# Sample retention outputs with the masked queries as weights, four column quarters side by side, instead of the states as weights

## The reference, cut to what matters

```python
def step(s, qkv):
    qc, kc, vc = qkv
    scores = jnp.einsum('bhid,bhjd->bhij', qc, kc) * decay_mat
    o = (jnp.einsum('bhij,bhjd->bhid', scores, vc)
         + jnp.einsum('bhid,bhde->bhie', qc * q_decay, s))
    ...
mu = jnp.mean(o, axis=-1, keepdims=True)
var = jnp.mean(jnp.square(o - mu), axis=-1, keepdims=True)
o = ((o - mu) * lax.rsqrt(var + GN_EPS)).reshape(B, L, R) * gn_g
ret_out = jax.nn.silu(g) * o
mix = jnp.concatenate([pool_out, ret_out], axis=-1) @ w_out
```

## Time and profile before

| | |
|---|---|
| median of 3 runs | 827.15 us (826.68 to 827.21) |
| span of the profiled execution | 823.5 us |
| its own time | not given on the page; the median of the runs is 3.65 us above its span |
| TensorE busy | 808.6 us, 98% |
| VectorE, ScalarE, POOL busy | 73%, 58%, 39% |
| DMA | 188.18 MB, mean 229 GB/s |

### The profile page before, as it was taken

How to read it: one execution, slowest core, us unless ns; L and a number is a source line. 1 busy time by engine, 2 the same in 40 slices (tenths; PEclk the granted TensorE clock), 3 DMA queues, 4 the chain that set the end, 5 groups by cost and what they waited for, 6 DMA issues and landing times.

```text
span 823.5 us, 11871 instructions
## 1 busy us (share of the span) xinstructions
PE 808.6 (98%) x4070; PEld 651.3 (79%) x4070; DVE 600.6 (73%) x957; ACT 478.4 (58%) x810; POOL 320.3 (39%) x207
## 2 busy tenths in 40 slices
PE   9999999999999999999999999999999999999995
PEld 6887788888868888888588887888878678888871
DVE  5444655645689999999854456555747899999986
ACT  5533342513478888887663432442334798888874
POOL 0016994301042345664100299913011322665540
PEclk9999999999999999999999999999999999999999
DMA  9732223223949999998853222221278699999867
GB/s 308 269 111 77 71 71 115 92 76 130 411 169 359 382 354 382 395 375 295 267 194 101 73 78 76 64 90 65 84 285 328 207 416 359 382 384 391 339 234 281
DMA packets 57295, 188.18 MB, mean 229 GB/s; under 512 B 10862, under 2 KB 11886, under 8 KB 49036
## 3 DMA queue, kind: packets, MB, share of 16 engines
q1 hardware_dynamic: 44476, 156.57, 52.5%
q0 software_dynamic: 10368, 23.09, 7.6%
q10 hardware_dynamic: 2400, 7.87, 2.5%
HBM read 173.00 MB, written 29.39 MB: 246 GB/s over the span
## 4 chain that ended last, share of the span: by engine, by line
PE 90%; DVE 4%; DMA 3%; issue 1%; ACT 1%; POOL 0%; ACTq 0%; SPq 0%; POOLq 0%; DVEq 0%
PE ps L485 13%; PE ps L1455 12%; PE ps L1457 12%; PE ps L1456 12%; PE ps L489 10%; PE ps L488 10%; PE ps L1463 3%; PE ps L487 3%; PE ps L1434 2%; PE ps L1654 1%; PE ps L1715 1%; DMA hg<-xn_d,rowidx 1%; PE ps L1679 1%; PE ps L1694 1%; PE ps L1405 1%
## 5 line engine op out<-in xcount | busy, mean ns | idle before, releaser
L485 PE MATMUL ps<-wh,hT 128*128 128x512 f32 x408 | 163.5, 401 | 0.2
L898 POOL DMA_INDIRECT y_d<-y,rowidx x32 | 111.8, 3493 | 125.8 <-DVE y L2179 124.5
L2154 DVE TENSOR_TENSOR gul<-wgu,eh 128x1024 fp32r<-128x1024 f32 x128 | 150.1, 1212 | 0.1
L2145 DVE SCALAR_TENSOR_TENSOR wl<-raw,gcol,wh 128x512 fp32r<-128x512 f32 x80 | 78.5, 984 | 75.3 <-ACT wh L1107 75.2
L1138 ACT ACTIVATE eh<-wgu 128x1024 fp32r<-128x1024 f32 x128 | 128.4, 1058 | 3.7 <-PE ps L1457 3.7
L489 PE MATMUL ps<-wh,lT 128*128 128x512 f32 x313 | 122.4, 391 | 0.0
L488 PE MATMUL ps<-wl,hT 128*128 128x512 f32 x313 | 121.9, 390 | 0.0
L1455 PE MATMUL ps<-eh,hgTh 128*128 128x512 f32 x240 | 96.6, 403 | 0.4 <-issue 0.4
L1457 PE MATMUL ps<-eh,hgTl 128*128 128x512 f32 x240 | 93.9, 391 | 0.0
L1456 PE MATMUL ps<-gul,hgTh 128*128 128x512 f32 x240 | 93.6, 390 | 0.0
L1107 ACT ACTIVATE wh<-raw,gcol 128x512 fp32r<-128x512 f32 x80 | 57.3, 719 | 59.8 <-PE ps L487 57.6
(11 more groups left out here) (271 smaller groups left out, 1688.2 us busy)
## 6 DMA issues: line engine op xcount, KB each, us to landing
wgu<-in_gate_up SPq DMA_DIRECT2D x64, 1024.0 KB, 12.4
wdn<-in_w_down SPq DMA_DIRECT2D x64, 512.0 KB
raw<-in_w_in SPq DMA_DIRECT2D x79, 256.0 KB, 2.7
raw<-in_w_out SPq DMA_DIRECT2D x32, 256.0 KB, 2.9
back<-y_d SPq DMA_DIRECT2D x16, 512.0 KB, 5.5
s<-in_state_ret POOLq DMA_DIRECT2D x8, 512.0 KB, 4.0
xn_d<-xf ACTq DMA_DIRECT2D x8, 512.0 KB, 6.6
x_in<-in_x_cols SPq DMA_DIRECT2D x8, 288.0 KB, 5.2
```

The costliest lines, as they stand in the source:

```text
L485: pe.matmul(out, both, w_h, start=first, stop=False)
L898: pool.indirect_dma_start(out=y_d, out_offset=bass.IndirectOffsetOnAxis(ap=rowidx[:, 1, e:e + 1], axis=0), in_=y[s][:, :], in_offset=None, ...
L2145: ve.scalar_tensor_tensor(out=wl[S % SPL][:, :], in0=raw[S % RAW][:, :], scalar=gcol[:, 0, L, s % KC:s % KC + 1], in1=wh[S % SPL][:, :].bi ...
L2154: ve.tensor_tensor(gu_pair(gul, gul3, e, s, p), gu_pair(wgu, wgu3, e, s, p), gu_split(e, p)[:, :].bitcast(F32), ALU.subtract).then_inc(glo, 1)
```

## The change

The operands are swapped. Now the states stream (128 columns) and the queries are the stationary operand. To keep sequences apart, POOL builds qm: for each head and each half (32 tokens, 4 sequences) a strip of 160 zeros in which four groups of 8 query columns stand 40 apart. A window of 32 columns at 32b holds the queries of sequence b of the half at their own place and zeros elsewhere, so four products by four states add up in one output of 32 rows. A pair of heads with two halves each makes four such outputs; they go to partitions 0, 32, 64 and 96 of bank B_OT, 128 columns a pair of heads. The scores' product has the score tile (32 columns) as stationary operand and v streaming. The four outputs are taken in turn for each b.

The output then is in natural layout, tokens down. The copy on ScalarE and the transposes back are gone. Statistics take two instructions of each kind instead of four, on a tile that has heads 0 and 2 in rows 0 to 63 and heads 1 and 3 in rows 64 to 127; the norm writes them as 64 rows of four heads. The table gneps is arranged to match, and rows 64 to 127 of on[LAST] are zeroed once.

```diff
--- before.py
+++ after.py
@@ -87,6 +87,9 @@
     def row_eps(chunk):
         return EPS_GN * np.exp(-2.0 * ((p % chunk) + 1.0).astype(f)[:, None] * log_g[None])
 
+    def by_half(rows):
+        return np.concatenate([np.where(p[:, None] < NSAMP, rows[:, 0::2], rows[:, 1::2])] * 2, 1)
+
     def kdecay(chunk):
         return np.exp((chunk - 1.0 - (p % chunk)).astype(f)[:, None] * log_g[None]) * scale
 
@@ -106,7 +109,7 @@
         "decay": np.stack([decay(P), decay(DECS)], 1),
         "cosT": np.concatenate([np.cos(ang)[:, :LAST]] * 2, 2).transpose(2, 1, 0),
         "sinT": np.concatenate([np.sin(ang)[:, :LAST], -np.sin(ang)[:, :LAST]], 2).transpose(2, 1, 0),
-        "gneps": np.stack([row_eps(P), row_eps(DECS)], 1),
+        "gneps": np.stack([row_eps(P), by_half(row_eps(DECS))], 1),
         "kdec": np.stack([kdecay(P)] + [kdecay_sample(0 if L + 1 < NL else LATE) for L in range(NL)], 1),
         "seqm": seq_mask,
         "least": np.broadcast_to(np.where(valid > 0, f(3.5), f(9))[:, :, None], (P, NT, NG)),
@@ -184,6 +187,7 @@
         hT = tile("hT", [P, KC, TOK], F32R, off=region)
         lT = tile("lT", [P, KC, TOK], F32R, off=region + 20 * 1024)
         xT = tile("xT", [P, KC, TOK], off=region)
+        qm = tile("qm", [P, 2, 4, 160], off=region)
         hg = [tile(f"hg{i}", [P, D], off=region + 4096 * i) for i in range(3)]
         y = [tile(f"y{i}", [P, D], off=region + 4096 * (3 + i)) for i in range(3)]
         hgTh = tile("hgTh", [P, KC, P], F32R, off=region + 4096 * 6)
@@ -389,6 +393,14 @@
         def q_turned(h, t):
 
             return qT[:, h, 0:NSAMP] if t == LAST else z[:, h, OFFS["q"], t * P:(t + 1) * P]
+
+        def own_queries(h, half):
+
+            return qm[:, h // 2, 2 * (h % 2) + half, :].rearrange("p (b s) -> p b s", s=40)[:, :, 0:DECS]
+
+        def masked_queries(h, half, b):
+
+            return qm[:, h // 2, 2 * (h % 2) + half, 32 * b:32 * b + 32]
 
         def keys_there(L, t):
 
@@ -925,13 +937,21 @@
                 pool.wait_ge(zmm, 5 * NT * (L + 1))
                 for h in range(2, NH):
                     load_s0(L, h)
-
-                for t in range(NT):
+                link(pool.memset(qm[:, :, :, :], 0.0))
+
+                for t in range(2):
+                    gate_gain(L, t)
+                pool.wait_ge(qk_ev, keys_there(L, LAST))
+                for h in range(NH):
+                    for half in range(2):
+                        last = pool.tensor_copy(own_queries(h, half), qT[:, h, 32 * half:32 * half + 32].rearrange("p (b s) -> p b s", s=DECS))
+                last.then_inc(qm_done, 1)
+                for t in range(2, NT):
                     gate_gain(L, t)
                 for h in range(LATE, NH):
                     if h == 2:
                         pool.wait_ge(sg_done, NT * (L + 1))
-                        pool.wait_ge(o_back, L + 1)
+                        pool.wait_ge(o_mm, NT * L + LAST)
                     if h == 3:
                         pool.wait_ge(on_tr, NT * L + 5)
                     pool.tensor_tensor(vb[h][:, :, :], over(zq(LAST, "v")[:, h * P:(h + 1) * P], DECB),
@@ -1304,8 +1324,6 @@
                     w_hi(L, s)
                 sc.wait_ge(st_ready, LAST * (L + 1))
                 sc.dma_start(o["new_ret_prompt"][L], st[:, :, :]).then_inc(st_st, 16)
-                sc.wait_ge(o_mm, NT * (L + 1))
-                sc.activation(scT[1][:, :, :], heads(ps[B_OT][:, :]), ACT.Copy).then_inc(o_ev, 1)
                 w_hi(L, WIN_STEPS + 8)
                 o_hi(sc, L, 0)
                 o_hi(sc, L, 1)
@@ -1700,21 +1718,29 @@
                     last = pe.matmul(ps[B_KV][:, h * P:(h + 1) * P], kd[t % 2][:, h, :], zq(t, "v")[:, h * P:(h + 1) * P], start=True, stop=True)
                 last.then_inc(kv_mm, 1)
 
-            def sample_part(L, h, part):
-
-                out = ps[B_OT][:, h * P:(h + 1) * P]
-                if h == 0 and part == 0:
+            def sample_heads(L, hp):
+
+                if hp == 0:
                     pe.wait_ge(sc_ev, NT * (L + 1))
                     pe.wait_ge(kd_done, NT * (L + 1))
                     for t in (2, 3, LAST):
                         z_there(pe, L, 4, t)
-                if part == 0:
+                    pe.wait_ge(qm_done, L + 1)
+                for h in (2 * hp, 2 * hp + 1):
                     pe.wait_ge(s0_ld[h], 16 * (L + 1))
-                    pe.matmul(out, zq(LAST, "v")[:, h * P:(h + 1) * P], scT[0][:, h, :], start=True, stop=False)
-                for b in (2 * part, 2 * part + 1):
-                    last = pe.matmul(out[:, b * DECS:(b + 1) * DECS], s0[h][:, b, :], qT[:, h, b * DECS:(b + 1) * DECS],
-                                     start=False, stop=(b == DECB - 1))
-                if h == NH - 1 and part == 3:
+                quarters = [(h, half) for h in (2 * hp, 2 * hp + 1) for half in range(2)]
+
+                def out(h, half):
+
+                    at = NSAMP * (h % 2) + 32 * half
+                    return ps[B_OT][at:at + 32, hp * P:hp * P + P]
+
+                for h, half in quarters:
+                    pe.matmul(out(h, half), scT[0][:, h, 32 * half:32 * half + 32], zq(LAST, "v")[:, h * P:(h + 1) * P], start=True, stop=False)
+                for b in range(4):
+                    for h, half in quarters:
+                        last = pe.matmul(out(h, half), masked_queries(h, half, b), s0[h][:, 4 * half + b, :], start=False, stop=(b == 3))
+                if hp:
                     last.then_inc(o_mm, 1)
 
             def late_old(L, h, n):
@@ -1738,13 +1764,6 @@
                 for n in range(2):
                     last = pe.matmul(ps[B_END[L][h][n]][:, :], kv_end[0:NSAMP, h, :], vb[h][0:NSAMP, 4 * n:4 * n + 4, :], start=not old, stop=True)
                 last.then_inc(skv_mm, 1)
-
-            def back(L):
-
-                pe.wait_ge(o_ev, L + 1)
-                for h in range(NH):
-                    last = pe.transpose(ps[B_OT][:, h * P:(h + 1) * P], scT[1][:, h, :], ident)
-                last.then_inc(o_back, 1)
 
             def own_rows(t):
 
@@ -1811,20 +1830,19 @@
                 for t in range(NT):
                     for i in range(4):
                         wout_mm(L, i, t)
-                        if t >= 2:
-                            sample_part(L, t - 2, i)
                     if t == 0:
                         qk_t(L, LAST)
                     elif t == 1:
                         scores(L, LAST)
                         outputs(L, 3)
+                    elif t == 3:
+                        sample_heads(L, 0)
                 for i in range(4, 2 * KC - SPL):
                     for t in range(NT):
                         wout_mm(L, i, t)
-                        if i == 4 and t < LAST:
-                            sample_part(L, 3, t)
+                    if i == 4:
+                        sample_heads(L, 1)
                     if i == 5:
-                        back(L)
                         on_t(pe, L, 0)
                         on_t(pe, L, 1)
                     if i == 6:
...
+            ve.memset(on[LAST][NSAMP:P, :, :], 0.0)
@@ -2275,19 +2294,14 @@
                 ve.wait_ge(sc_mm, T + 1)
                 ve.tensor_tensor(scT[t % 2][:, :, :], heads(ps[B_SC][:, :]), c("decay", 2, NH)[:, int(t == LAST), :, :], ALU.mult).then_inc(sc_ev, 1)
 
-            def o_bank(t):
-                return ps[B_O if t < LAST else B_OT]
-
             def group_stats(L, t):
 
-                if t < LAST:
-                    ve.wait_ge(o_mm, NT * L + t + 1)
-                else:
-                    ve.wait_ge(o_back, L + 1)
-                for h in range(NH):
-                    last = ve.bn_stats(bnst[:, h, :], o_bank(t)[:, h * P:(h + 1) * P])
+                ve.wait_ge(o_mm, NT * L + t + 1)
+                bank, n = (ps[B_O], NH) if t < LAST else (ps[B_OT], NH // 2)
+                for h in range(n):
+                    last = ve.bn_stats(bnst[:, h, :], bank[:, h * P:(h + 1) * P])
                 link(last)
-                for h in range(NH):
+                for h in range(n):
                     last = ve.bn_aggr(mv[:, h, :], bnst[:, h, :])
                 link(last)
                 ve.scalar_tensor_tensor(out=gnv[:, :], in0=c("gneps", 2)[:, int(t == LAST), :], scalar=msq[:, t:t + 1], in1=mv[:, :, 1],
@@ -2313,7 +2327,12 @@
                 ve.wait_ge(gn_rt, T + 1)
                 link(ve.reciprocal(gnrs[:, :], gnrt[:, :]))
                 for h in range(NH):
-                    last = ve.tensor_scalar(on[t][:, h, :], o_bank(t)[:, h * P:(h + 1) * P], mv[:, h, 0:1], gnrs[:, h:h + 1], ALU.subtract, ALU.mult)
+                    if t < LAST:
+                        rows, i, bank = slice(0, P), h, ps[B_O]
+                    else:
+                        rows, i, bank = slice(NSAMP * (h % 2), NSAMP * (h % 2) + NSAMP), h // 2, ps[B_OT]
```

(9 more changed lines are left out.)

## The result

| | before | after |
|---|---|---|
| median of the runs, us | 826.91 (826.65 to 827.21, 4 runs) | 814.97 (814.37 to 816.40, 4 runs) |
| span of the profiled execution, us | 823.5 | 812.8 |

The ratio is 0.9865, with an interval from 0.9852 to 0.9877: the kernel became 12 us faster. The direction was right and the size was not.

A forecast was written before the change was run, and what follows sets the result against it. TensorE, busy 98% of the span, was taken as the bound. Per layer 8.5 us go and 4.4 + 0.55 + 0.25 = 5.2 come, saving 3.3, 6.6 in all: 827.15 - 6.6 = 820.5 us, range 816.5 to 829.5.

The forecast's parts named there:

- What goes: TensorE in each layer: sample parts 7.2 us, L1713 products 0.9, transposes back 0.44; together 8.5 us removed.
- The products: TensorE, two blocks a layer: one product every 0.11 us, 0.055 a pair, so 40 products add 4.4 us a layer.
- The load of 0.041 a pair: TensorE blocks: load time of a 32 wide stationary, extended in a straight line from 128 and 64 wide pairs.
- Rival A: TensorE blocks: quarters stream at once and only loads bind, 3.3 us a layer for products, 818.3 us; chance 0.20.
- floor of 0.025: TensorE blocks: no pair below 0.025 us, from bf16 pairs; products 2.0 us a layer, 815.7 us, left outside the range.
- B: TensorE blocks: loads not hidden under another quarter's stream, products 6.0 us a layer, 823.7 us; chance 0.15.
- C: TensorE blocks: quarters do not stream at once, products 8.8 us a layer, 829.3 us, slower; chance 0.13.
- D: TensorE blocks: each load waits until every running matmul has ended, products 12.0 us a layer, 835.7 us; chance 0.05.
- E: POOL's copies late or slot wait above 0.25 us; each us counts once a layer; chance 0.05 with anything else.
- The switch: TensorE around each block: changing between wide and 32 wide stationaries costs 0.28 us a block, 0.55 a layer.
- The slot wait: W_out step 4, last tile: TensorE waits for the weight slot step 0 frees, about 0.25 us a layer.
- POOL, VectorE, ScalarE: Beside TensorE: POOL's memset and copies finish 8 us before needed; VectorE and ScalarE savings count nothing.

The follow-up runs named there:

- e1: Changed kernel with the same 20 products a block, but one column quarter after the other: 823.16 us, ratio to before 0.9962.
- e2: Changed kernel with all four outputs of a block added up in the first 32 partitions, so one column quarter (sample retention wrong): 829.01 us.
- e3: Changed kernel with both blocks of a layer together, between the last tile's W_out steps 3 and 4: 813.47 us, ratio to before 0.984.
- after_again: Changed kernel unaltered, run once more in the same series: 815.68 us, ratio to before 0.9858.
- e8: Changed kernel with two products of one quarter in a row before the next quarter has its two: 814.21 us.
- e7: Changed kernel with two quarters at a time, the two halves of one head in turn, then the other head: 817.17 us.
- e9: Changed kernel with three products of one quarter in a row, then the other two: 817.19 us.
- e5: First kernel with its sample parts gathered into two blocks a layer, at the places of the changed kernel's blocks: 833.39 us.

## Why the prediction was wrong

**What goes, 8.5 us a layer: right.** It was read from distances between starts, and the 5.34 us less from scores to transposes are what it leaves after the 3.24 that came.

**The products, 4.4 us a layer: the step that failed.** It is the sentence "The next product's first half can then run beside this one's second half, but not earlier", with its reason that all starts are in program order. The measured figure is 1.09 us a block and 2.2 a layer, 0.027 a pair instead of 0.055. In e1 a half starts ahead of three that stand before it in the program. In the changed kernel the first four halves of a block, one of each quarter, start 7 ns apart (168.333, 168.340, 168.346, 168.352). The next four start from 168.466 on, 133 ns after them, and from then on four start together every 109 ns: four streams at once, where the argument allowed two. In the first kernel the output of every narrow product begins at partition 0 (L1679 and L1654 too), so no two matmuls there lay in quarters wholly apart, and the order of its starts could not bear the argument.

**The ends.** The load of 0.041 a pair, read from 128 and 64 wide loads, was no bound either: the loads of four quarters start a few ns apart too. Rival A was thus right that the halves of a product don't hold up the next quarter (in a row of up to four), and wrong that loads then bind. Its floor of 0.025, which I wrote off because its row was bf16, was nearly reached. That the two come so close is luck as far as the runs show: here 0.027 is 0.109 us shared by four quarters, which is not what the bf16 row measured. With the floor the sum was 815.7, against 814.97; by the spans 10.7 us went, and it had 11.4. The range was too narrow at this end: it left out a bound of its own.

**Rivals B, C, D and E.** B fell: it would have made a block 3.3 us long. C fell, and e2 shows what it would have cost. D fell too: its rule would have made a block some 6 us long. The Trainium skill, "TensorE: Matmul & The Clock Gate", Part 3, The mechanism, has a load overlap a running matmul only where the row group differs, and matmuls start strictly in program order; in this case loads overlap with all quarters on the same rows, and e1's 169.06 is out of order. The measurement decides. Of E the copies were early and the slot wait was 0.1 longer.

**The switch, 0.28 a block: near.** It is 0.34: the 0.09 in front came out as read, inside the block 0.14 instead of 0.09, behind it 0.11 instead of 0.10.

**The slot wait, 0.25 a layer: right in kind.** It is 0.28, and 0.10 more because the product behind a standstill also starts late, which the sum did not hold. e3 shows it as a wait that a block in the right place covers.

**POOL, VectorE, ScalarE: right.** POOL in order of time, changed kernel:

```profile
157.96 1.25 POOL L947 COPY qm<-qT 128x32 f32<-128x32 f32 x8 [2.42 <-ACT kT L1250]
159.18 3.72 POOL L896 TENSOR_TENSOR z<-z,gnrow 128x512 f32<-128x512 f32 x3
```

The copies end at 159.2, 9 us before the first block; nobody waits for them. Behind W_out little of the gain was lost: the transposes of the second layer start 10.87 us earlier, and the span ends 10.7 earlier. On the way 0.4 is lost up to the first experts of that layer, where this trace has a fall of the granted clock to 0.79 (624 to 632 us), and 0.60 in the last expert, where TensorE waits for VectorE and VectorE for a load; the first kernel waits 0.55 for a load a little later (810.64), which the changed one does not.

In one line: 2 x (8.5 - 2.2 - 0.68 - 0.38) = 10.5 us, where the forecast had 2 x (8.5 - 4.4 - 0.55 - 0.25) = 6.6. The difference is the product term, 4.4 us, less 0.5 for switches and wait. The two profiled spans differ by 10.7 and the medians by 11.9. The rest is in the 3.65 us that the prediction put around the span: in every run whose time and span are both known, 1.7 to 1.8 us lie around it. By that the profiled execution of the first kernel was some 1.8 us shorter than the median of its runs, and a difference of medians holds such scatter too; against the runs beside it, after_again gains 11.0.

## What to carry to other kernels

Products with few output rows belong side by side in different 32 column quarters: four of them took the time of one, as long as no more than four halves (two f32 products) of a quarter stood in a row (e8). When a step rests on the order in which things were seen to start, ask whether the trace could have shown another order at all; where it couldn't, the bound that the other order gives belongs inside the range. Keep products of the same width together in few groups (0.34 us each here), and put a group where it covers a wait.

## What was not expected of the hardware

- Starts of matmuls in different quarters need not be in program order (e1), and a quarter holds three waiting halves while others go on (rule W, within 0.05 us a block in e1, e7, e8, e9).
- Gathered blocks of 36 halves, 32 of them with only 8 columns streaming and TensorE at 4.00 busy of 4, were followed by a fall of the granted clock from 1.00 to 0.50 for some us in three cases of four (e5, one run). The same work spread among 512 column products in the first kernel kept 1.00. Single falls stand in other traces too, but not at the blocks (0.79 in 624 to 632 us of the changed kernel, 0.71 in 228 to 232 of e9). What distinguishes the block that kept 1.00 was not tried.
